# The sums of weights of a two-level matrix product, moved from VectorE to accumulating transfers

## The reference, cut to what matters

```
def rms_norm(x, g):
    return x * rsqrt(mean(x * x) + EPS) * g

def swiglu(h, wg, wu, wd):          # wg, wu: 1024 x 2816   wd: 2816 x 1024
    return (silu(h @ wg) * (h @ wu)) @ wd

for layer in range(2):
    x = x + 0.5 * swiglu(rms_norm(x), ...)     # feed-forwards 0 and 2
    x = x + mixer(rms_norm(x))                 # attention with a convolution; pooling
    x = x + 0.5 * swiglu(rms_norm(x), ...)     # feed-forwards 1 and 3
```

## Time and profile before, and how to read it

| | |
|---|---|
| median of three runs | 1689.89 us |
| the profiled execution's own time | 1690.82 us |
| its span in the trace | 1689.0 us |
| TensorE (PE) busy | 1674.9 us, 99% |
| VectorE (DVE) busy | 1285.5 us, 76% |
| ScalarE (ACT) busy | 753.4 us, 45% |
| GpSimd (POOL) busy | 121.2 us, 7% |
| granted TensorE clock | full over the whole span |
| DMA engines | 30.8% by SyncE's queue, 165.05 MB, 98 GB/s |

### The profile page before, as it was taken

How to read it: one execution, slowest core, us unless ns; L and a number is a source line. 1 busy time by engine, 2 the same in 40 slices (tenths; PEclk the granted TensorE clock), 3 DMA queues, 4 the chain that set the end, 5 groups by cost and what they waited for, 6 DMA issues and landing times.

```text
span 1689.0 us, 25810 instructions
## 1 busy us (share of the span) xinstructions
PE 1674.9 (99%) x10644; PEld 1492.2 (88%) x10644; DVE 1285.5 (76%) x1466; ACT 753.4 (45%) x1008; POOL 121.2 (7%) x115
## 2 busy tenths in 40 slices
PE   8999999999999999999999999999999999999999
PEld 7899999987876688999999889999998889999997
DVE  6977877767788658887877687877876798778774
ACT  7434435443237555444434464434434644344341
POOL 0010300032014220000000200000001000000000
PEclk9999999999999999999999999999999999999999
DMA  7422422162420034332421443422411334224212
GB/s 219 141 85 76 150 76 87 63 149 71 102 66 26 14 100 138 112 113 75 131 95 38 126 125 101 138 87 76 150 38 65 106 117 147 79 76 149 75 58 68
DMA packets 180924, 165.05 MB, mean 98 GB/s; under 512 B 15396, under 2 KB 156680, under 8 KB 180808
## 3 DMA queue, kind: packets, MB, share of 16 engines
q1 hardware_dynamic: 179960, 162.79, 30.8%
q10 hardware_dynamic: 848, 0.61, 0.2%
HBM read 160.89 MB, written 2.10 MB: 96 GB/s over the span
## 4 chain that ended last, share of the span: by engine, by line
PE 92%; DVE 5%; issue 1%; ACT 1%; DMA 0%; SPq 0%; DVEq 0%; ACTq 0%
PE ps_s L747 19%; PE ps_s L749 19%; PE ps_s L748 19%; PE ps_y L747 6%; PE ps_y L748 6%; PE ps_y L749 6%; PE ps_stat L747 2%; PE ps_aux L747 2%; PE ps_aux L749 2%; PE ps_stat L749 2%; PE ps_aux L748 2%; PE ps_stat L748 2%; PE ps_s L1153 1%; PE ps_y L1182 1%; PE ps_aux L1202 1%
## 5 line engine op out<-in xcount | busy, mean ns | idle before, releaser
L747 PE MATMUL ps_s<-xg_hi,w_hi 128*128 128x256 f32 (+1 forms) x1280 | 409.7, 320 | 1.3 <-DVE w_lo L1793 1.3
L749 PE MATMUL ps_s<-xg_hi,w_lo 128*128 128x256 f32 (+1 forms) x1280 | 406.6, 318 | 0.0
L748 PE MATMUL ps_s<-xg_lo,w_hi 128*128 128x256 f32 (+1 forms) x1280 | 406.6, 318 | 0.0
L1793 DVE TENSOR_TENSOR w_lo<-raw,w_hi 128x1024 fp32r<-128x1024 f32 (+2 forms) x210 | 252.8, 1204 | 135.9 <-ACT w_hi L1333 135.7
L747 PE MATMUL ps_s<-xt_hi,w_hi 128*128 128x256 f32 x1152 | 326.2, 283 | 2.1 <-ACT pair_gu L1333 2.1
L748 PE MATMUL ps_s<-xt_lo,w_hi 128*128 128x256 f32 x1152 | 326.0, 283 | 0.0
L749 PE MATMUL ps_s<-xt_hi,w_lo 128*128 128x256 f32 x1152 | 326.0, 283 | 0.0
L1333 ACT CAST w_hi<-raw 128x1024 fp32r<-128x1024 f32 (+1 forms) x212 | 217.7, 1029 | 183.6 <-PE ps_s L749 78.3
L747 PEld LDWEIGHTS ps_s<-xg_hi,w_hi 128*128 128x128 f32 x1280 | 243.9, 191 | 21.2 <-issue 3.5
L748 PEld LDWEIGHTS ps_s<-xg_lo,w_hi 128*128 128x128 f32 x1280 | 243.9, 191 | 18.6 <-issue 1.4
L749 PEld LDWEIGHTS ps_s<-xg_hi,w_lo 128*128 128x128 f32 x1280 | 243.8, 190 | 16.5
(11 more groups left out here) (369 smaller groups left out, 2386.3 us busy)
## 6 DMA issues: line engine op xcount, KB each, us to landing
scratch<-in_ffn_w_down SPq DMA_DIRECT2D x64, 512.0 KB, 4.7
raw<-in_ffn_w_gate SPq DMA_DIRECT2D x48, 512.0 KB, 4.0
raw<-in_ffn_w_up SPq DMA_DIRECT2D x48, 512.0 KB, 6.1
raw_b<-in_ffn_w_gate SPq DMA_DIRECT2D x40, 512.0 KB, 4.9
raw_b<-in_ffn_w_up SPq DMA_DIRECT2D x40, 512.0 KB, 6.9
raw<-in_hyb_w_in SPq DMA_DIRECT2D x18, 512.0 KB, 3.8
raw<-in_ffn_w_down SPq DMA_DIRECT2D x8, 768.0 KB, 5.5
raw_b<-in_ffn_w_down SPq DMA_DIRECT2D x8, 768.0 KB, 5.3
```

The costliest lines, as they stand in the source:

```text
L747: mm(bank, hi, x_hi, start=first, stop=False, **kw)
L748: mm(bank, hi, x_lo, start=False, stop=False, **kw)
L749: return mm(bank, lo, x_hi, start=False, stop=last, **kw)
L1793: tt(shaped(weight(w_lo, n, 0, BLOCKS[n] * P)), source, shaped(f32(weight(w_hi, n, 0, BLOCKS[n] * P))), ALU.subtract).then_inc(lo_ready, 1)
```

## The change

For steps 3 to 10 of each feed-forward (eight of nine), the four sums are no longer VectorE's. ScalarE negates a21 in place and writes -a22 into s1 (`negate`), after which every sum is a plain addition onto a block in place, and GpSimd's queue issues it as a transfer from SBUF to SBUF that accumulates (`form_sums`): s1 += -a21; a21 (now -a21) += a11; a11 += s1 (its sign is turned); a12 += the new a11. Each of the four waits for the one before to have landed (`s_summed`), the third also for the split of form 0, the fourth for that of form 1. The signs that come out differently are taken up by the other operand: two of the four differences of x are turned (`x_forms`). For step 2 VectorE still makes the sums, with the new signs. So that the rows of the transfers are 4 KB, a quarter now lies in one piece of 1024 elements a partition (`quarter_row`), and each load of a step is cut in two: eight loads of 256 KB with rows of 512 B in place of four of 512 KB with rows of 1 KB. GpSimd's angle reductions of feed-forward 0 are placed after the sums of steps 4 and 6.

```
+def summed_by(ffn, s, count):
+
+    return 16 * (4 * ((STEPS - 1) * ffn + s - FIRST - 1) + count)
...
+        def quarter_row(s, a, kh):
+
+            return step_at(s)[:, (2 * a + kh) * WP:(2 * a + kh + 1) * WP]
+
         def quarter(s, a, kh):
 
-            return step_at(s).rearrange("p (m k c) -> p m k c", m=2, k=KD)[:, :, 4 * kh:4 * kh + 4, a * P:(a + 1) * P]
+            return as_form(quarter_row(s, a, kh))
...
-                columns = slice(s * 2 * P, (s + 1) * 2 * P)
                 for m, name in enumerate(("ffn_w_gate", "ffn_w_up")):
                     for kh in range(2):
-                        first = (m * KD + 4 * kh) * 2 * P
-                        sp.dma_start(step_at(s)[:, first:first + KD * P].rearrange("p (k c) -> p k c", k=4),
-                                     blocks_of(A[name][ffn // 2, ffn % 2][4 * kh * P:4 * (kh + 1) * P, columns])
-                                     ).then_inc(step_landed[(s - FIRST) % 2], 16)
+                        for a in range(2):
+                            f = (2 * s + a) * P
+                            sp.dma_start(quarter(s, a, kh)[:, m, :, :],
+                                         blocks_of(A[name][ffn // 2, ffn % 2][4 * kh * P:4 * (kh + 1) * P, f:f + P])
+                                         ).then_inc(step_landed[(s - FIRST) % 2], 16)
...
-                    if m in MADE_AS:
-                        act.wait_ge(s_made, 4 * q_of(ffn, s) + MADE_AS[m])
+                    if m in MADE_AS and s == FIRST:
+                        act.wait_ge(s_made, 4 * ffn + MADE_AS[m])
+                    elif m in MADE_AS:
+                        act.wait_ge(s_summed, summed_by(ffn, s, MADE_AS[m]))
...
+            def negate(ffn, s):
+
+                act.wait_ge(step_landed[(s - FIRST) % 2], step_landed_by(ffn, s))
+                a21 = quarter_row(s, 1, 0)
+                nc.scalar.activation(a21, a21, ACT.Copy, scale=-1.0).then_inc(negated, 1)
+                act.wait_ge(lo_ready, u_form(ffn, s - 1, 3) + 1)
+                if s - 1 == FIRST:
+                    act.wait_ge(s_made, 4 * ffn + 3)
+                else:
+                    act.wait_ge(s_summed, summed_by(ffn, s - 1, 3))
+                nc.scalar.activation(s1, quarter_row(s, 1, 1), ACT.Copy, scale=-1.0).then_inc(negated, 1)
...
                 split(n + 6)
+                if s < LAST:
+                    negate(ffn, s + 1)
                 split(n + 7)
...
-            def sum_2(ffn, s):
-
-                dve.wait_ge(lo_ready, u_form(ffn, s, 0) + 1)
-                dve.wait_ge(s_made, 4 * q_of(ffn, s) + 2)
-                a11 = quarter(s, 0, 0)
-                tt(a11, as_form(s1), a11, ALU.subtract).then_inc(s_made, 1)
...
                 split(n + 5)
-                if s < LAST:
-                    sum_1(ffn, s + 1)
                 split(n + 6)
-                if s < LAST:
-                    sum_3(ffn, s + 1)
...
                     product(q)
-                    sum_2(ffn, s + 1)
                     pair_low(ffn, s)
                     add_half(ffn, s - FIRST, 0)
                     split(n + 10)
-                    sum_4(ffn, s + 1)
...
+            def form_sums(ffn, s):
+
+                q = (STEPS - 1) * ffn + s - FIRST - 1
+
+                def add(dst, source):
+                    pool.dma_start(dst, source, accum_op=ALU.add).then_inc(s_summed, 16)
+
+                pool.wait_ge(negated, 2 * q + 2)
+                add(s1, quarter_row(s, 1, 0))
+                pool.wait_ge(s_summed, summed_by(ffn, s, 1))
+                add(quarter_row(s, 1, 0), quarter_row(s, 0, 0))
+                pool.wait_ge(s_summed, summed_by(ffn, s, 2))
+                pool.wait_ge(lo_ready, u_form(ffn, s, 0) + 1)
+                add(quarter_row(s, 0, 0), s1)
+                pool.wait_ge(s_summed, summed_by(ffn, s, 3))
+                pool.wait_ge(lo_ready, u_form(ffn, s, 1) + 1)
+                add(quarter_row(s, 0, 1), quarter_row(s, 0, 0))
```

More of the change, by code:

```diff
@@ L105, in step_landed_by @@
 def step_landed_by(ffn, s):
-    each = 64 * len(range(FIRST + (s - FIRST) % 2, LAST + 1, 2)) + 32
-    return ffn * each + 64 * ((s - FIRST) // 2 + 1)
+    each = 128 * len(range(FIRST + (s - FIRST) % 2, LAST + 1, 2)) + 32
+    return ffn * each + 128 * ((s - FIRST) // 2 + 1)
+def summed_by(ffn, s, count):
+    return 16 * (4 * ((STEPS - 1) * ffn + s - FIRST - 1) + count)
 def half_landed_by(ffn, h):
@@ L429, in build @@
         s_made = sem("s_made")
+        s_summed = sem("s_summed")
+        negated = sem("negated")
         snapped = sem("snapped")
@@ L1838, in x_forms_low, with sum_1, sum_3, sum_2 @@
                    ALU.subtract).then_inc(xt_lo_ready, 1)
[L1840 to L1850, removed]
-            def sum_2(ffn, s):
-                dve.wait_ge(lo_ready, u_form(ffn, s, 0) + 1)
-                dve.wait_ge(s_made, 4 * q_of(ffn, s) + 2)
-                a11 = quarter(s, 0, 0)
-                tt(a11, as_form(s1), a11, ALU.subtract).then_inc(s_made, 1)
[L1859 to L1864, removed]
+            def sum_1(ffn):
+                dve.wait_ge(step_landed[0], step_landed_by(ffn, FIRST))
+                dve.wait_ge(lo_ready, U_FFN[ffn] + 8)
+                stt(s1, quarter_row(FIRST, 1, 0), -1.0, quarter_row(FIRST, 1, 1), ALU.mult, ALU.subtract).then_inc(s_made, 1)
+            def sum_3(ffn):
+                dve.wait_ge(s_made, 4 * ffn + 1)
+                a21 = quarter_row(FIRST, 1, 0)
+                tt(a21, quarter_row(FIRST, 0, 0), a21, ALU.subtract).then_inc(s_made, 1)
+            def sum_2(ffn):
+                dve.wait_ge(lo_ready, u_form(ffn, FIRST, 0) + 1)
+                dve.wait_ge(s_made, 4 * ffn + 2)
+                a11 = quarter_row(FIRST, 0, 0)
+                tt(a11, a11, s1, ALU.add).then_inc(s_made, 1)
+            def sum_4(ffn):
+                dve.wait_ge(lo_ready, u_form(ffn, FIRST, 1) + 1)
+                dve.wait_ge(s_made, 4 * ffn + 3)
+                a12 = quarter_row(FIRST, 0, 1)
+                tt(a12, a12, quarter_row(FIRST, 0, 0), ALU.add).then_inc(s_made, 1)
             def first_pairs(ffn, version):
@@ L1936, in first_pairs @@
                 gate_of(2)
-                sum_1(ffn, FIRST)
-                sum_3(ffn, FIRST)
+                sum_1(ffn)
+                sum_3(ffn)
                 up_of(2)
@@ L1941, in first_pairs @@
                 product_of(2)
-                sum_2(ffn, FIRST)
+                sum_2(ffn)
                 low_of(2)
@@ L1945, in first_pairs @@
                 split(n + 9)
-                sum_4(ffn, FIRST)
+                sum_4(ffn)
                 up_of(3)
@@ L2465, in _, with turn_angles @@
             then(nc.gpsimd.memset(cos_t[:, T:TE], 0.0))
-            pool.wait_ge(angle_ready, 1)
-            for many, steps_done in ((1024.0, 2), (1.0, 4)):
-                pool.wait_ge(turn_lo_ready, steps_done)
+            def form_sums(ffn, s):
[12 more added lines that the diff above has]
+                add(quarter_row(s, 0, 1), quarter_row(s, 0, 0))
+            def turn_angles(many):
                 then(ts(turns, ang, 1.0 / (2 * np.pi * many), ROUND, ALU.mult, ALU.add))
@@ L2475, in _ @@
                     then(tt(ang, ang, step_, ALU.subtract))
-            ts(ang, ang, 3.1415925, -3.1415925, ALU.min, ALU.max).then_inc(turn_ready, 1)
+            for s in range(FIRST + 1, LAST + 1):
+                form_sums(0, s)
+                if s == FIRST + 2:
+                    pool.wait_ge(angle_ready, 1)
+                    turn_angles(1024.0)
+                if s == FIRST + 4:
+                    turn_angles(1.0)
+                    ts(ang, ang, 3.1415925, -3.1415925, ALU.min, ALU.max).then_inc(turn_ready, 1)
             sums(1)
@@ L2542, in _, with all_form_sums @@
                         split_low(U_OUT + j)
+            def all_form_sums(ffn):
+                for s in range(FIRST + 1, LAST + 1):
+                    form_sums(ffn, s)
             sums(2)
+            all_form_sums(1)
             sums(3)
+            all_form_sums(2)
             sums(4, KD - 1)
+            all_form_sums(3)
 _INS = ["x", "positions", "ffn_norm", "ffn_w_gate", "ffn_w_up", "ffn_w_down", "mix_norm", "hyb_w_in", "hyb_q_norm",
```

6 lines of the change are left out of this document (3 added, 3 removed).

## The result

The changed kernel takes 1747.45 us (median of four, 1747.22 to 1755.72) against 1689.84 us: a ratio of 1.0348, with an interval of 1.0335 to 1.036. It is 57.6 us slower. The forecast's likeliest case, no change at 1690 us, did not come about; the rival in which the chain of transfers is a little late did (priced at 1725 to 1773). The time lies in the stated range of 1686.5 to 1810 only because that range had been drawn wide enough to take in this rival; the sum itself gave the chain no cost.

A forecast was written before the change was run, and what follows sets the result against it. TensorE, busy 99% of the span, was taken to set the pace, with VectorE only following. Terms of 0 for VectorE, ScalarE, loads and chain on 1690.8 us gave a forecast of 1690 us, range 1686.5 to 1810.

The forecast's parts named there:

- no change: Whole kernel: nothing given back and no stall in the 32 changed steps, 1690 us; chance 0.45.
- a little late: TensorE before form 2 of steps 3 to 10: three transfers exceed 19.0 us, time 1725 to 1773 us; chance 0.32.
- The faster rival: TensorE's waits on ScalarE and VectorE all go, up to 3.4 us won, 1686.5 us; chance 0.03.
- VectorE: VectorE loses 128 sums of 1.22 us, 156 us, falling from 1285.5 to about 1129 us; gain for the kernel 0.
- ScalarE: ScalarE gains two negations a step, 67 us, from 753 to about 820 us; cost 0.
- The loads: SyncE's queue: eight loads with 512 B rows take 7.3 us of engines instead of 5.5, issues 4 us; cost 0.
- The chain of transfers: GpSimd's queue: three dependent transfers before form 2 take 16.4 us of 19.0, slack 2.6 us, stall 0.
- The room: From the first transfer's issue at 231.2 to the split of form 2 at 250.2: 19.0 us for three transfers.
- no contention: Three transfers with the DMA engines to themselves, 4.6 us each, take 13.8 us.
- equal shares: Both queues share the DMA engines equally while both have work: three transfers take 19.0 us, no slack.
- side branch: Each transfer's GpSimd preparation waits for a 1.22 us VectorE instruction: 20.1 us for three, stall 1.1 us a step, 1725 us.
- The accumulation is slow: Addition halves the transfers' data rate once more: 8.5 us each, stall 6.5 us a step, 1898 us; chance 0.20.

The follow-up runs named there:

- the four runs back at 1691 us: Changed kernel with loads behind the third transfer, 1690.89 us; additions on VectorE, 1691.08; plain copies, 1690.97; late loads, earlier negations and split angle reductions, 1690.63.
- four placements tried: Changed kernel with all loads behind the third transfer, 1690.89 us; only down weights there, 1748.34; only quarters there, 1743.15; only down weights behind the fourth, 1707.28.

## Why the prediction was right or wrong

*What bounds the kernel.* Right. With 141 to 145 us taken from VectorE and nothing put in TensorE's way, the time does not move (1690.63 and 1690.89). The faster rival, up to 3.4 us, did not come true; the waits of the earlier trace rows stay.

*VectorE.* 1144 us for the 1129 predicted. The 1.22 us of the earlier trace rows overlap the next instruction by about a tenth of a microsecond (the instruction behind the one at 237.26 in the earlier trace rows starts 1.14 us later), so 128 sums were worth 141, not 156 us.

```profile
238.40 1.22 DVE L1979 TENSOR_TENSOR work<-pair_gu 128x1024 f32<-128x1024 f32 x1
```

*ScalarE.* Cost 0, right (shown by the run with the additions on VectorE). 804 us for 820: the overlap takes about 6 us (64 times a tenth); in the four runs back at 1691 us ScalarE has 810 to 815 us, and what else makes the 804 is open.

*The loads.* Cost 0 for their own sake, right, in the same run. With rows of 512 B they move 0.33 MB in the microsecond from 248 and 0.29 MB in that from 256, near the 286 GB/s taken. Their issue was mis-sized: eight were to take 4 us and took 8.6 (246.32 to 254.88), so the down weights are issued at 254.93, 0.3 us ahead of the second transfer. What the loads do to the chain is the next point.

*The chain of transfers.* The forecast failed here, and in one term. The room, 19.0 us, was right: it is 19.1 in 25 steps, and the step shown is late by 21.2 - 19.0 = 2.2 us, and TensorE waits 2.2. The price alone, 4.6 us, was right: 4.6 to landing, 4.8 to the next issue. The doubled data time was right too: the engines move 0.20 MB/us of sums against 0.40, and a copy without the addition takes 1.6 us less, where 1.3 was expected. The Trainium skill's sentence that the second read is what an add costs (Collectives: The Full Stack, reduce-scatter) agrees with these rows nearly in full, but they show only the doubled time, which an addition at half the rate would give as well.

What was mis-sized is the company of the loads. The prediction took 16.4 us, the middle between no contention (13.8) and equal shares (19.0), with the argument that long rows should not fare worse than short ones. They do not (the run with short rows), but that gives no middle. Measured are 20.0 us at the median and 21.2 in the step shown, beyond the end that was thought to be the worst. Equal shares comes near in the sum, with 7.2, 7.2 and 4.6 us against 7.3, 7.8 and 4.6, but partly by luck, since the rows do not show it: the loads hold a copy up as long as an addition, and 1 MB of them at least as long as 2 MB. What fits the runs is a wait of 2.5 to 3.4 us at every link that has a burst of loads beside it, again and again because the next transfer is issued only when the one before has landed.

The Trainium skill (DMA: Bandwidth & Descriptors, Queues, rings and completion order) has an engine switch between queues packet by packet, of 9 to 17 descriptors as a rule. That alone does not give this wait. In the microseconds from 257 and 258 the loads moved 422 and 194 packets, 38 for each of the 16 engines and more than one such turn, and the transfer issued at 255.24 moved none; the third, alone, was issued at 263.88 and moved its first data in the microsecond from 265. Whether the transfer is held up at the engines or in its preparation, no run here separates.

*The rivals.* "A little late" was the right mechanism at the right place, before form 2 of steps 3 to 10, with 29 new waits for 32 steps; its prices of 35 and 83 us hold the 57.6 between them. The 83 had all three transfers at 7.2 us; in the trace two are slower than that and the third, alone, takes 4.6. Its side branch, that GpSimd's preparation waits for VectorE, was not needed: alone the transfers take 4.8 us with VectorE busy 68% of the span (the run with late loads). "The accumulation is slow" fell. What no rival had was GpSimd's own work in front of the chain, 6.8 us of waits in the changed kernel and 12.5 us in the version with early negations, and TensorE's clock, which by its mean costs 10 us on top of the waits: the prediction priced a stall at its own length.

*The chances.* No change had 0.45, slower 0.52 in two pieces. The text gave slower the larger sum but forecast no change as the single likeliest. With the loads taken as a wait at every link they stand beside, "a little late" would have been the likeliest.

## What to carry to other kernels

Before work is moved from an engine to a chain of dependent transfers, write down the room from the first issue to the first reader and price every link beside the loads that are issued in that stretch, since here each burst beside a link cost its own wait, 2.5 to 3.4 us, whatever the link moved. If loads have slack and the chain has none, put the loads behind it with one wait, and then look at what the loads are wanted for and which transfer they now stand in front of: of four placements tried, one gave back all of the 57 us, one 40, and two almost nothing. Price the other work of the engine that issues the chain as well. And here an engine that was not the bound gave nothing back when it was relieved of 141 to 145 us.

## What the runs showed of the hardware that was not expected

- Two queues on the same DMA engines shared them unevenly, by turns: in the step shown, from 247 to 262, every microsecond in which both moved data gave one queue at least three quarters of the 16 engines' time, and for the three from 255 to 257 the loads had it alone (112% to 121%) with a transfer issued.
- A copy of 512 KB within SBUF from GpSimd's queue takes 3.2 us from issue to next issue and an accumulating one 4.8; beside loads, by the medians of 32 chains, 5.7 and 6.6 (first and second copy) and 7.3 and 7.8 (first and second addition).
- TensorE's granted clock fell to 0.50 for some 3 us with six of the 29 new waits, among them one of 1.9 us, and did not fall with others of 2.2 and 2.4 us; in such a stretch (from 236.3) a product of 256 columns started every 0.21 us instead of every 0.12.
- The GpSimd instruction of the earlier trace rows took 1.50 us both times it ran before the change and 2.34 us both times after it (133.3 and 201.9), with VectorE at work in the same stretches in both kernels. Why is open.
